# Four weight slots moved 64 bytes further apart in a float32 decoder layer on one Trainium2 core

## The reference, cut to what matters

```
u   = rmsnorm(x, mix_norm_g) @ w_in        # 1024 -> about 10,000 columns
a   = mlstm(...); b = short_conv_mixer(...); c = mamba2_mixer(...); d = stick_breaking_attention(...)
m   = sum over the four of sigmoid(gate_i) * (branch_i @ w_lift[i])   # 512 -> 1024 each
x   = x + m @ w_out                        # 1024 -> 1024
h   = causal_dwconv(rmsnorm(x, ffn_norm_g) @ w_up, conv_w) + conv_b   # 1024 -> 5632
x   = x + (silu(g) * u) @ w_down           # 2816 -> 1024
out = rmsnorm(x, final_norm_g)
```

## Time and profile before

| | |
|---|---|
| time of two executions | 1037.99 and 1036.34 us, median 1037.16 us |
| profiled execution | 1038.42 us; span from first to last instruction 1036.7 us |
| PE busy | 1019.0 us (98%), 4724 matmuls |
| PEld busy | 837.8 us (81%), 4724 weight loads |
| DVE busy | 593.2 us (57%) |
| ACT busy | 424.3 us (41%) |
| POOL busy | 67.6 us (7%) |
| mean granted TensorE clock | 0.992 of full |

### The profile page before, as it was taken

The page is one execution under the profiler, slowest core; times in us unless marked ns, Lnnn a source line. Parts: engine busy times, 40 slices in busy tenths (PEclk is TensorE's granted clock), DMA queues, the critical chain, the costliest instruction groups (busy, mean ns, idle before and its releaser), DMA issues.

```text
span 1036.7 us, 12635 instructions
## 1 busy us (share of the span) xinstructions
PE 1019.0 (98%) x4724; PEld 837.8 (81%) x4724; DVE 593.2 (57%) x764; ACT 424.3 (41%) x515; POOL 67.6 (7%) x74
## 2 busy tenths in 40 slices
PE   8999999999999999999999999989999999999996
PEld 7897888887777887777888888868888888888886
DVE  6835754656676566556364456687656666543323
ACT  5514445644435322444432333544444344332331
POOL 5610000000000000000000000320000000000002
PEclk9999999999999999999999999989999999999998
DMA  6332222223222333343252222513233222253312
GB/s 238 114 113 70 82 84 82 77 93 105 89 85 82 120 122 124 132 132 103 81 183 87 97 88 97 181 61 119 85 100 101 100 86 88 68 176 94 102 56 81
DMA packets 32024, 108.24 MB, mean 104 GB/s; under 512 B 3684, under 2 KB 5860, under 8 KB 31600
## 3 DMA queue, kind: packets, MB, share of 16 engines
q1 hardware_dynamic: 29520, 93.86, 27.1%
q0 software_dynamic: 2320, 13.69, 4.0%
q10 hardware_dynamic: 144, 0.14, 0.1%
HBM read 103.42 MB, written 4.25 MB: 104 GB/s over the span
## 4 chain that ended last, share of the span: by engine, by line
PE 93%; DVE 4%; ACT 2%; issue 1%; DMA 1%; DVEq 0%; SPq 0%; ACTq 0%
PE gb L413 81%; PE gb L446 4%; DVE w_lo L985 1%; PE xb L596 1%; PE gb L524 1%; PE xb L556 1%; PE xb L549 1%; PE xb L536 1%; PE xb L413 1%; ACT w_hi L701 1%; PE xb L513 1%; DMA raw<-w_stream 1%; DVE y_lo L993 1%; PE gb L464 1%; PE xb L584 0%
## 5 line engine op out<-in xcount | busy, mean ns | idle before, releaser
L985 DVE TENSOR_TENSOR w_lo<-raw,w_hi 128x1024 fp32r<-128x1024 f32 (+2 forms) x181 | 218.1, 1206 | 342.8 <-ACT w_hi L701 342.4
L701 ACT ACTIVATE w_hi<-raw 128x1024 fp32r<-128x1024 f32 (+2 forms) x181 | 183.8, 1017 | 413.5 <-PE gb L413 380.8
L413 PE MATMUL gb<-xn_hi,w_hi 128*128 128x512 f32 x720 | 285.0, 396 | 0.0
L413 PE MATMUL gb<-xn_hi,w_lo 128*128 128x512 f32 x720 | 281.1, 390 | 0.0
L413 PE MATMUL gb<-xn_lo,w_hi 128*128 128x512 f32 x720 | 281.0, 390 | 0.0
L413 PE MATMUL gb<-y_hi,w_hi 128*128 128x512 f32 x400 | 159.1, 398 | 6.0 <-DVE y_lo L993 4.2
L413 PEld LDWEIGHTS gb<-xn_hi,w_hi 128*128 128x128 f32 x720 | 135.8, 189 | 29.7 <-issue 1.0
L413 PEld LDWEIGHTS gb<-xn_lo,w_hi 128*128 128x128 f32 x720 | 135.8, 189 | 29.0 <-issue 1.4
L413 PEld LDWEIGHTS gb<-xn_hi,w_lo 128*128 128x128 f32 x720 | 135.6, 188 | 28.6
L413 PE MATMUL gb<-y_lo,w_hi 128*128 128x512 f32 x400 | 156.6, 391 | 0.0
L413 PE MATMUL gb<-y_hi,w_lo 128*128 128x512 f32 x400 | 156.4, 391 | 0.0
(11 more groups left out here) (231 smaller groups left out, 1018.4 us busy)
## 6 DMA issues: line engine op xcount, KB each, us to landing
raw<-w_stream SPq DMA_DIRECT2D x149, 512.0 KB, 3.3
raw<-w_down SPq DMA_DIRECT2D x16, 384.0 KB, 3.0
abc<-scr_a POOLq DMA_DIRECT2D x8, 640.0 KB, 4.1
raw<-w_down SPq DMA_DIRECT2D x16, 320.0 KB, 2.8
x_in<-xT SPq DMA_DIRECT2D x8, 256.0 KB, 6.5
x<-xT POOLq DMA_DIRECT2D x1, 2048.0 KB, 8.5
scr_x<-x POOLq DMA_DIRECT2D x1, 2048.0 KB, 7.4
x<-scr_x POOLq DMA_DIRECT2D x1, 2048.0 KB, 8.4
```

Source lines behind the costliest of these rows:

```text
L413: ins = pe.matmul(out, w[:, r, lo:hi], rhs(k)[x], start=(first and n == 0 and q == 0), stop=(last_ and n == len(ks) - 1 and q == 2))
L701: act.activation(w_hi[:, r, 0:n], raw[:, r, 0:n], ACT.Copy).then_inc(S["hi_ready"], 1)
L985: dve.tensor_tensor(w_lo[:, r, 0:n], raw[:, r, 0:n], w_hi[:, r, 0:n].bitcast(F32), ALU.subtract)\
```

## The change

`w_hi` and `w_lo` are allocated with 16 elements (64 bytes) more for each slot, and the slice that is used leaves the padding out. A slot is still 4096 bytes of data, but slots lie 4160 bytes apart. After each of the two tiles the next address is rounded up to a multiple of 512 bytes from `base`, so that `w_lo`, `xn_hi` and all tiles behind them keep their place modulo 512 bytes (they move up by 512 and 1024 bytes). Slots 0, 1, 2 and 3 of `w_hi` and of `w_lo` thus start 0, 64, 128 and 192 bytes from the activation tiles modulo 512. `raw` is not touched. No instruction is added, removed or put elsewhere on any engine, and none reads or writes more; only addresses differ.

```diff
@@ -43,6 +43,7 @@
 LINE = 512
+STEP = 16
@@ -151,8 +152,11 @@
     m = Map(base)
     raw = m.put("raw", [P, RING, 1024])
-    w_hi = m.put("w_hi", [P, RING, 1024], F32R)
-    w_lo = m.put("w_lo", [P, RING, 1024], F32R)
+    w_hi = m.put("w_hi", [P, RING, 1024 + STEP], F32R)[:, :, 0:1024]
+    m.at = base + (m.at - base + LINE - 1) // LINE * LINE
+    w_lo = m.put("w_lo", [P, RING, 1024 + STEP], F32R)[:, :, 0:1024]
+    m.at = base + (m.at - base + LINE - 1) // LINE * LINE
+    X0 = m.at
     xn_hi = m.put("xn_hi", [P, KD, T], F32R)
     xn_lo = m.put("xn_lo", [P, KD, T], F32R)
@@ -235,7 +239,7 @@
-    x2 = at("x2", [P, KD, T], F32, base + 3 * RING * 4096)
+    x2 = at("x2", [P, KD, T], F32, X0)
```

## The result

The changed kernel takes 1050.52 us (median of two runs, 1050.23 and 1050.81) against 1037.16 us, a ratio of 1.0129 (95% interval 1.0085 to 1.0172). Timed again, with the medians of four and of seven runs, it gave 1050.07 against 1037.42 us, a ratio of **1.0125 (1.0108 to 1.0142)**. The forecast was 1046.7 us: the direction is right. The loss that was forecast, 9.5 us, is a quarter short of the 12.7 us of the second measurement and 29% short of the 13.4 us of the first.

A forecast was written before the change was run, and what follows sets the result against it. PE's matmul pitch was taken as the bound; 1038.42 us profiled plus 9.5 us for 2877 shifted matmuls gave 1047.9, and 1046.7 us with the median 1.3 us lower. The main case spanned 1040 to 1056 us, the range 1012 to 1066 us.

The forecast's parts named there:

- The bound: Whole kernel: the pitch at which matmuls follow one another on PE sets the end, 226.6 ns, 13.3 ns of it not streaming.
- The step that carries the forecast: 512-column matmuls in slots 1 to 3: weights off the streamed tile's place modulo 512 keep pitch at 230.0 ns, +9.5 us.
- unit 12: Unit whose weight loads read 96 columns instead of 128, same streamed tile; its 230.0 ns pitch was taken as the price.
- The disturbed state: Pitches just after an interruption, mean 231 ns over ten matmuls from 302.33 to 304.64 us, before settling at 226.6.
- The signs: Expected in the profile after: about 1311 matmuls between 700 and 1000 us; units in slots 1 to 3 take 5.52 us.
- Slot 0: Unshifted slot: units should stay at 226.7 ns, 5.44 us for 24 matmuls; a change would mean rhythm carried from neighbours.
- The reversed units: Units 8 to 11 and 17 to 20, shifted slot streamed: 288 matmuls of 256 columns, +1.0 to -1.0 us, taken as zero.
- the last halves: Last output tile, computed in halves, 102 matmuls in slots 1 to 3: +-0.3 us, taken as zero.
- DVE, ACT, DMA: Subtraction and copy on shifted slots: covered, zero with up to +1 us where DVE is full; DMA: nothing.
- No change: Rival, 30%: the fixed part is timing alone, or only place within a block smaller than 64 bytes counts; 1037 us.
- Faster: Rival, 20%: load and stream meet in one memory bank, shifting avoids it; half the fixed part gone 1018 us, all 998.
- Much slower: Rival, 17%: the stream must catch up with and pass a load 64 to 192 bytes ahead; 236 ns pitch, 1064 us.

## Why the prediction was nearly right

*The bound.* PE's pitch sets the end, and the waits that feed it don't: right, they moved by 0.6 us.

*The step that carries the forecast,* "a load that doesn't fit keeps the rhythm out of" its settled state, was right in kind. The runs with only the activations moved and with both moved show that the settled 226.7 ns needs the common place; it is modulo 256 bytes and not 512, which makes no difference for shifts of 64 to 192. The chance of one in three for it was low for how plainly the disturbed pitches spoke, but no row before the change showed an address at work.

*Its size* was too small. I priced all three slots at 230.0, by unit 12; they had 233.2, 232.4 and 229.8, in the mean 231.8. The 2877 matmuls cost 14.1 us in place of 9.5. Unit 12 was a poor measure: its 230.0 belongs to 96 columns at place 0, and it moves to 231.8 and 226.7 when the place alone changes. Had its slot lain 112 bytes off before, the row would have shown no extra at all, so it is in part luck that it pointed the right way and near the size. The disturbed state, 231 ns over ten matmuls, was the better row: it would have given (231 - 226.7) x 2877 = 12.4 us. The total came nearer than this term, since the 256-column matmuls and the longer intervals gave back 0.95 and 0.9 us that the sum did not have.

*The signs* came as written, with the larger size: 1302 matmuls between 700 and 1000 us for 1311, and units of 5.59, 5.58 and 5.51 us for 5.52. The three shifted slots differ, so the distance matters and one price for three was too coarse.

*Slot 0* kept its pitch after the first three matmuls of a unit, which take 228 to 233 ns in units 120 and 124: +0.4 us in all from the neighbour's rhythm carried over, as I had named it and not counted it.

*The reversed units* I took at zero between -1.0 and +1.0, and the last halves at zero within 0.3; together they gave -0.95 us (-1.2 in the second profile), most of the bound on the fast side. The same shifts that cost a 512-column stream 3 to 6 ns give the reversed units' 256-column streams 1 to 5 back (120.5 ns at 0; 118.7, 118.6 and 116.1 in slots 1 to 3).

*DVE, ACT, DMA:* zero, and zero they were: 1263 and 1058 ns, and 32024 DMA packets with 108.24 MB in both profiles.

*The rivals.* No change: it needed that only the place within a block smaller than 64 bytes counts, or that addresses play no role. The slots at 64 to 192 bytes rule out both. The Trainium skill, page "SBUF — State Buffer" (section "Specifications (TRN2)"), has lines of 16 bytes; a shift of 16 keeps every start on the start of a line, and it costs 6.2 ns here (233.3 for 227.1), so that rule did not cover this. Faster: none of the fifteen distances brought the pitch under 226.7. That load and stream start together at one place is the best state tried, not the collision I had described. Much slower: 236 as the lasting pitch of a slot was not reached in any kernel; 234.3 at 96 bytes is the highest mean, though single pitches in the steady cycles go to 241. The picture of a stream stuck behind its load isn't borne out: by it I would expect 64, 128 and 192 bytes to cost in the order of the distance, and 4 bytes next to nothing.

The Trainium skill, page "TensorE: Matmul & The Clock Gate" (section "Part 2: What happens when you issue a matmul"), says that a load takes nothing from the running matmul's reads. By it the change is free. Here the weights' place alone makes a matmul 4.9 ns longer in the mean of three slots, so for this format and length the measurement decides against it. Whether it is the reads that meet, or something that times them, no run here tells.

## What to carry to other kernels

When PE is without a gap, read the pitch from start times and compare it with columns over clock; a remainder that varies from unit to unit is worth a look at addresses. For float32r matmuls of 512 columns with a fresh load of 128 columns each, keep all weight tiles and streamed tiles at one place modulo 256 bytes: each kernel here that left it was 1.2 to 2.2% slower, and a slot that is off by a single column has a pitch 2% longer. Here an unseen alignment was better priced by a disturbed stretch of the same shape than by a steady one of another.

## What the hardware showed that I had not expected

- The dependence has a period of 256 bytes and a grain no coarser than 4: the runs with slots at 0 to 192 and 256 to 448 bytes agree to 0.1 ns in each slot, and 4 bytes cost 5 ns.
- Off the common place the pitches run through fixed cycles: 236 and 231 in turn in slot 1 of the changed kernel, 226, 229 and 232 in its slot 3, fifteen values with the low halves off, and a level 233.3 when all are 64 bytes off.
- With 256 columns the common place is not the best. The reversed units have 120.5 ns at 0, 115.0 to 116.1 at 192 and 114.9 at 112 bytes, but 123.3 at 4. For their 384 matmuls the best would be some 2.2 us (384 x 5.6 ns, an estimate); it needs those units' weights at another place than the rest in the same slots, and wasn't tried.
- With 256 columns one place can have more than one rhythm: slot 1 of the reversed units has 118.7 ns in the first profile of the changed kernel and 116.5 in the second.
